# A decoder step on one core: input stage rebuilt, norm factor applied at the copy out, sample rows of v in column groups

## The chip, the cores and the metric

The kernel runs on one core of a Trainium2 chip. The time is that of the device, in microseconds (us), from one execution of the whole program. Engines are TensorE (PE), VectorE (DVE), ScalarE (ACT), GpSimd (POOL) and SyncE (SP), which here only issues DMAs. Times on the timeline are counted from the profiled execution's first instruction.

## The reference, cut to what matters

One step of two decoder layers in fp32, for a prompt of 512 tokens and 8 samples of one token with 1024 cached positions each. Only the start of layer 0 is touched:

```python
hn = rmsnorm(h, norm_mix[0])            # x * rsqrt(mean(x*x) + eps) * gain, 1024 channels
proj = hn @ w_in_ab                     # 1024 x 2048: q, k, v, u, 512 columns each
past_k = cache_k[:, page_table]         # 8 samples x 8 pages of 128 positions, 8 heads x 64
o_sb = stick_breaking_attention(q, [past_k, k], [past_v, v])
pooled = trailing_means(u, widths 2, 4, 8, 16) - u
```

k, v and the last rows of u are outputs too. Then come the output projection, a mixture of 16 experts, a gated embedding, a layer with a convolution of 31 taps (`w_dw`) and a second mixture.

## The kernel before, in words

**Layout.** Channels lie on the 128 partitions: `hT` holds the residual as 8 blocks (`k`) of 128 channels by 520 tokens (512 of the prompt, 8 of the samples). `xnT` holds the normalised one. Large weights and cache pages pass through six ring buffers ("units") of 2 MB. The first 22 units have fixed places: `w_in_ab` for q, k, u, v in buffers 0 to 3, the first two samples' keys in 4 and 5, the next keys in 0, 4, 5, and so on as uses end.

**PSUM.** Work that passes through PSUM is a list of jobs (`dense_plan`), each with the engine that copies it out. Job n uses slot n mod 4, and TensorE's `fill_wait` waits until job n - 4 is copied out. Every engine runs its program strictly in order; engines meet by semaphores.

**Input (before).** SP issues x_prompt in two halves, x_sample, eight page table transfers (each a strided column of 4 B elements for 16 partitions) and the first weight unit, then waits for all twelve small ACT transfers before it issues units 1 to 3. VectorE computes the row numbers for the cache gathers from the page table (L1252 to L1255) and then copies the transposed x out of PSUM (L1260, L1262). TensorE turns x, then the parameter rows and the 31 tap rows (L1816 to L1825).

**Norm (before).** ScalarE squares `hT` block by block into two buffers (L899), VectorE adds (L1236), TensorE sums over partitions (L1782), ScalarE takes the root (L907), VectorE the reciprocal (L1244) and then forms `xnT` = `hT` x gain x factor (L1247). Only then can the products start.

**Projections.** Each of q, k and u is four channel blocks of 8 x 2 products 128x128x260 (L1804), copied out by ScalarE (L890). v is computed with tokens on the output rows (L1872): 16 products of 512 columns for each of two jobs and 8 for the samples' rows. The q rows of the samples are turned, written to DRAM (L709) and read back broadcast over the partitions (L705). For each sample VectorE multiplies the gathered keys with that (L1283) and reduces them (L1286), in the order keys 0 to 4, pooling history and pooling (L1294 to L1301), keys 5 to 7. GpSimd issues the gathers (L683) and the q broadcasts in one program order; each gather waits until the buffer's last user is done.

**Attention.** For each head ScalarE scales the scores, VectorE starts the chain at L1354, GpSimd masks, and TensorE sums the sticks (L1905). `keep_busy` (L1768) are products whose result nobody reads, ahead of some waits.

## Time and profile before

| | us |
|---|---|
| median of 3 runs | 1443.25 (1442.7 to 1445.9) |
| the profiled execution: its time | 1447.69 |
| the profiled execution: its span, first to last instruction | 1445.9 |
| busy: PE, DVE, ACT, POOL | 1338.9, 1015.4, 709.1, 255.2 |
| mean granted TensorE clock | 0.965 |

A busy TensorE is not one at its peak: matmul ends are modelled and overlap. The granted clock is a share of the full 2.4 GHz, so 0.50 is 1.2 GHz. An idle engine costs something only where the chain passes through it.

### The profile page before, as it was taken

Reading aid. Unit: us, or ns where it says so; the run is one execution under the profiler, and the core shown is the slowest. Engines: PE = TensorE matmul, PEld = TensorE weight load, DVE = VectorE, ACT = ScalarE, POOL = GpSimd, SP = SyncE. Lnnn points to the kernel's source line nnn. Section 1 sums busy time; section 2 is a strip of 40 time slices with the busy share of each in tenths; the row PEclk is TensorE's granted clock in tenths of the full one; section 3 lists DMA queues with packets and bytes.
Section 4 is the critical chain, followed back from the end, with each engine's and each line's share of the span. In section 5 each row is a group of like instructions: output and inputs, shape, how many; then the busy total and the mean of one; then the engine's idle time right before and its main releaser. Section 6 shows DMA issues by size and latency. Waiting matters only on the chain.

```text
span 1445.9 us, 16284 instructions
## 1 busy us (share of the span) xinstructions
PE 1338.9 (93%) x6237; PEld 1046.7 (72%) x6238; DVE 1015.4 (70%) x1038; ACT 709.1 (49%) x702; POOL 255.2 (18%) x251
## 2 busy tenths in 40 slices
PE   2899988999799999998999999999789999999897
PEld 2787454687678888887678885478678878887776
DVE  3258955314798888895855999932788888988573
ACT  2010144113577777774542007242467777877364
POOL 2034235300112332221000000100202233221000
PEclk7899999998999999999999999999899999999898
DMA  7539436306589999996542303002479999997401
GB/s 263 197 143 369 183 122 236 116 1 243 189 312 377 308 381 377 375 380 238 189 155 101 117 0 121 3 1 79 140 249 372 388 309 388 385 376 271 173 1 60
DMA packets 122726, 314.07 MB, mean 217 GB/s; under 512 B 10044, under 2 KB 10704, under 8 KB 120592
## 3 DMA queue, kind: packets, MB, share of 16 engines
q1 hardware_dynamic: 106942, 251.95, 48.0%
q0 software_dynamic: 13648, 56.56, 10.9%
q10 hardware_dynamic: 2074, 4.71, 1.0%
q8 instruction: 43, 0.70, 0.2%
q14 instruction: 19, 0.16, 0.0%
HBM read 304.17 MB, written 26.70 MB: 229 GB/s over the span
## 4 chain that ended last, share of the span: by engine, by line
PE 39%; DVE 9%; DMA 2%; issue 1%; ACT 1%; SPq 0%; ACTq 0%; POOLq 0%; DVEq 0%; PEldq 0%
PE ps L1804 12%; PE ps L2038 6%; PE ps L2039 5%; PE ps L2040 5%; DVE arena L1696 4%; PE ps L2192 2%; PE ps L2194 2%; PE ps L2193 2%; PE ps L1760 2%; DMA ring<-in_w_gate_e 2%; DVE ring_parts L1519 1%; DVE hT L1632 1%; PE ps L2309 1%; PE ps L2204 1%; DVE ring L1600 1%
## 5 line engine op out<-in xcount | busy, mean ns | idle before, releaser
L1804 PE MATMUL ps<-xnT,ring 128*128 128x260 f32 x1408 | 313.0, 385 | 7.3 <-DVE xnT L1247 5.1
L1804 PEld LDWEIGHTS ps<-xnT,ring 128*128 128x128 f32 x1408 | 268.5, 191 | 50.5 <-issue 5.8
L2039 PE MATMUL ps<-ring_parts,arena_parts 128*128 128x512 f32 x768 | 304.3, 396 | 0.0
L1519 DVE TENSOR_TENSOR ring_parts<-ring,xnT_parts 128x2048 fp32r<-128x2048 f32 x96 | 218.7, 2290 | 42.9 <-ACT xnT_parts L1012 41.7
L1519 DVE TENSOR_TENSOR ring_parts<-ring,arena_parts 128x2048 fp32r<-128x2048 f32 x96 | 218.9, 2289 | 32.8 <-ACT arena_parts L1012 32.1
L1012 ACT ACTIVATE xnT_parts<-ring 128x2048 fp32r<-128x2048 f32 x96 | 182.6, 1916 | 80.0 <-PE ps L2040 60.2
L1012 ACT ACTIVATE arena_parts<-ring 128x2048 fp32r<-128x2048 f32 x96 | 182.4, 1916 | 62.2 <-PE ps L2040 43.0
L2039 PEld LDWEIGHTS ps<-ring_parts,arena_parts 128*128 128x128 f32 x768 | 146.0, 190 | 30.6
L2038 PE MATMUL ps<-xnT_parts,arena_parts 128*128 128x512 f32 x384 | 155.5, 405 | 7.4 <-DVE arena_parts L1523 7.3
L2038 PE MATMUL ps<-arena_parts 128*128 128x512 f32 x384 | 155.0, 404 | 7.1 <-DVE arena_parts L1545 3.8
L2040 PE MATMUL ps<-xnT_parts,arena_parts 128*128 128x512 f32 x384 | 152.7, 398 | 0.0
L2040 PE MATMUL ps<-arena_parts 128*128 128x512 f32 x384 | 150.9, 393 | 0.0
L788 POOL DMA_INDIRECT y_rows<-arena,tab_i x32 | 65.3, 2039 | 455.2 <-ACT arena L1024 455.2
L1696 DVE SCALAR_TENSOR_TENSOR arena<-arena,wdw 128x512 f32<-128x512 f32 x150 | 112.8, 752 | 6.0 <-DVE arena L1722 0.2
L1760 PE MATMUL ps<-ident,arena 128*128 128x128 f32 (+5 forms) x617 | 84.9, 283 | 28.9 <-DVE hT L1260 10.9
L783 POOL DMA_INDIRECT arena<-x_rows,tab_i x32 | 81.1, 2536 | 167.2 <-DMA x_rows<-arena 82.1
L1760 PEld LDWEIGHTS ps<-ident,arena 128*128 128x128 f32 (+5 forms) x617 | 74.7, 145 | 42.5 <-DVE hT L1260 12.8
L899 ACT ACTIVATE sq<-hT 128x520 f32<-128x520 f32 x56 | 35.1, 633 | 121.8 <-DVE hT L1405 90.2
L2038 PEld LDWEIGHTS ps<-xnT_parts,arena_parts 128*128 128x128 f32 x384 | 72.7, 189 | 25.9 <-DVE arena_parts L1523 9.0
L2038 PEld LDWEIGHTS ps<-arena_parts 128*128 128x128 f32 x384 | 72.8, 190 | 23.8 <-DVE arena_parts L1545 4.3
L2040 PEld LDWEIGHTS ps<-xnT_parts,arena_parts 128*128 128x128 f32 x384 | 72.7, 189 | 17.7
L2040 PEld LDWEIGHTS ps<-arena_parts 128*128 128x128 f32 x384 | 72.7, 189 | 17.2
(309 smaller groups left out, 1709.6 us busy)
## 6 DMA issues: line engine op xcount, KB each, us to landing
ring<-in_w_gate_e SPq DMA_DIRECT2D x32, 2048.0 KB, 18.3
ring<-in_w_up_e SPq DMA_DIRECT2D x32, 2048.0 KB, 17.6
ring<-in_w_down_e SPq DMA_DIRECT2D x32, 2048.0 KB, 18.9
ring<-in_w_in_ab SPq DMA_DIRECT2D x4, 2048.0 KB, 26.3
ring<-in_w_ple_gate SPq DMA_DIRECT2D x4, 2048.0 KB, 8.0
ring<-y_rows SPq DMA_DIRECT2D x16, 512.0 KB, 6.8
ring<-in_w_in_c SPq DMA_DIRECT2D x4, 2048.0 KB, 8.8
x_rows<-arena ACTq DMA_DIRECT2D x10, 416.0 KB
```

The lines of the kernel that those rows point to most:

```text
L783: pool.indirect_dma_start(xg[:, e % GATHERS, :], None, x_rows[layer], bass.IndirectOffsetOnAxis(ap=tab_i[:, 0, e * BLK:e * BLK + 1], axis= ...
L788: pool.indirect_dma_start(y_rows[layer], bass.IndirectOffsetOnAxis(ap=tab_i[:, 1, e * BLK:e * BLK + 1], axis=0), yo[:, e % 2, :], None, bo ...
L899: nc.scalar.activation(sq[:, k % 2, 0:T], src[:, k, :], ACT.Square).then_inc(s_sq, 1)
L1012: nc.scalar.activation(high[hu0 % 4], unit(n)[:, at:at + HU], ACT.Copy).then_inc(s_hi, 1)
L1519: v.tensor_tensor(w_lo, w, high[hu0 % 4].bitcast(F32), ALU.subtract).then_inc(s_lo, 1)
L1696: link(v.scalar_tensor_tensor(y, x, tap, y, ALU.mult, ALU.add))
L1760: return nc.tensor.transpose(dst, src, ident[0:n, 0:n])
L1804: ins = mm(s[:, half, 0:HALF], w[:, k, :], src[:, k, half * HALF:(half + 1) * HALF], start=(k == 0), stop=(k == n - 1))
L2038: mm(ps[:, bank, :], x, w, start=start, stop=False)
L2039: mm(ps[:, bank, :], x, w_lo, start=False, stop=False)
L2040: return mm(ps[:, bank, :], x_lo, w, start=False, stop=stop)
L2192: mm(s[:, 0, :], hi[:, k, cols], gx_hi[:, k, :], start=(k == 0), stop=False)
```

## The change

- The page table comes in one transfer of 256 B, broadcast to all 128 partitions, tenth on the ACT queue. Each partition picks its own page's column with a mask (`own_page`) and a sum, in fp32. This work now stands behind the copies of x on VectorE.
- x_sample goes first on SP's queue and its transposes come first. SP no longer waits before units 1 to 3. The constants that TensorE's transposes need come first on GpSimd.
- ScalarE squares each block as soon as its part of x is copied, into eight buffers (`sq8`); VectorE adds them in three operations. ScalarE also forms `xnT` = `hT` x gain, without the norm factor.
- TensorE starts the first q block on that, and takes the sums of the norm behind it, as columns for all tokens and as a value for each token row (`rtok`). VectorE applies the factor as it copies q, k and u out (`scaled`); ScalarE applies it for v.
- The taps are turned late, ahead of v. VectorE's key steps are split in two and interleaved with the copies. The first u block comes ahead of the k rows.
- The samples' rows of v are computed between the two other v jobs, as 8 products in four groups of 32 output rows, copied and folded by one more product.

```diff
-    order = [("x", i, "dve") for i in range(5)] + [("params", 0, "dve")]
+    order = [("x", i, "dve") for i in (4, 0, 1, 2, 3)] + [("params", 0, "dve")]
...
+    order.append(("q", 0, "dve"))
     norm(0)
-    order += [("q", m, "act") for m in range(4)] + [("qrow", 0, "act")]
-    order += [("k", m, "act") for m in range(4)] + [("krow", i, "act") for i in range(3)]
-    order += [("u", m, "act") for m in range(4)] + [("srow", 0, "act"), ("urow", 0, "dve")]
+    order += [("q", m, "dve") for m in range(1, 4)] + [("qrow", 0, "act")]
+    order += [("k", m, "dve") for m in range(4)] + [("u", 0, "dve")] + [("krow", i, "act") for i in range(3)]
+    order += [("u", m, "dve") for m in range(1, 4)] + [("srow", 0, "act"), ("urow", 0, "dve"), ("taps", 0, "dve")]
...
-        page_of = sb("page_of", [P, TS], I32)
+        page_all = sb("page_all", [P, TS * PAGES], I32)
+        page_f = sb("page_f", [P, TS * PAGES])
...
+        ar = Arena(8400)
+        sq8 = ar(KT, T)
...
+        vxs = shaped(arena[:, 15520:15776], (KT, 32))
+        vpart = arena[:, 12960:13472]
...
-                eng.wait_ge(s_drained["dve"], JOBS[("x", 4)][2])
+                eng.wait_ge(s_drained["dve"], JOBS[("x", k // 2)][2])
...
+            sp.dma_start(x_smp, a["x_sample"][:, 0, :]).then_inc(s_in, 16)
             sp.dma_start(x_tok[:, :, 0:D // 2], x_src[:, :, 0:D // 2]).then_inc(s_in, 16)
             sp.dma_start(x_tok[:, :, D // 2:D], x_src[:, :, D // 2:D]).then_inc(s_rest, 16)
-            sp.dma_start(x_smp, a["x_sample"][:, 0, :]).then_inc(s_rest, 16)
-
-            for g in range(PAGES):
-                sp.dma_start(page_of[SUB * g:SUB * g + SUB, :], a["page_table"][:, g].partition_broadcast(SUB),
-                             allow_slow_non_contiguous=True).then_inc(s_pt, 16)
             load(0)
-            sp.wait_ge(s_in2, 16 * 12)
             for n in range(1, 4):
                 load(n)
...
-            pool.iota(part_of[:], [[0, 1]], base=0, channel_multiplier=1).then_inc(s_part, 1)
             link(pool.memset(ones[:], 1.0))
             link(pool.memset(ident[:], 0.0))
             link(pool.affine_select(out=ident[:], in_=ident[:], compare_op=ALU.not_equal, fill=1.0, base=0,
                                     pattern=[[-1, P]], channel_multiplier=1))
+            link(pool.memset(eps[:], EPS))
+            pool.memset(idx[:], 0).then_inc(s_const, 1)
+            pool.iota(part_of[:], [[0, 1]], base=0, channel_multiplier=1)
...
+                               pattern=[[SUB, PAGES]], channel_multiplier=-1).then_inc(s_part, 1)
...
+            pool.iota(cfix[:], [[0, 4], [1, 16]], base=1, channel_multiplier=0,
+                      allow_small_or_imprecise_dtypes=True).then_inc(s_const, 1)
...
+            pool.memset(vxs, 0.0).then_inc(s_upz, 1)
             pool.dma_start(hist_rows, a["state_pool"][0].rearrange("b r c -> (b r) c")).then_inc(s_hist, 16)
...
-            act.dma_start(dw_rows, a["w_dw"][0]).then_inc(s_in2, 16)
-            act.dma_start(sbb[:], a["sb_bias"][0].partition_broadcast(P)).then_inc(s_in2, 16)
-            act.dma_start(wpool[:], a["w_pool"][0].rearrange("g c d -> c g d")).then_inc(s_in2, 16)
+            act.dma_start(page_all[:], a["page_table"].rearrange("b g -> (b g)").partition_broadcast(P)).then_inc(s_pt, 16)
+            act.dma_start(sbb[:], a["sb_bias"][0].partition_broadcast(P)).then_inc(s_in3, 16)
+            act.dma_start(wpool[:], a["w_pool"][0].rearrange("g c d -> c g d")).then_inc(s_in3, 16)
+            act.dma_start(dw_rows, a["w_dw"][0]).then_inc(s_in3, 16)
...
+            for k in range(KT):
+                h_wait(act, "x", k)
+                nc.scalar.activation(sq8[:, k, :], hT[:, k, :], ACT.Square).then_inc(s_sq, 1)
+            act.wait_ge(s_drained["dve"], JOBS[("params", 0)][2])
+            for k in range(KT):
+                nc.scalar.activation(xnT[:, k, :], hT[:, k, :], ACT.Copy, scale=prm[:, G_MIX + k:G_MIX + k + 1]
+                                     ).then_inc(s_xn, 1)
             act.wait_ge(s_const, 1)
-            norm(0, "x")
-            two = lambda t: t.rearrange("p (a b) -> p a b", a=2)
-            for m in range(4):
-                copy_out("q", m, two(qT[:, m, :]), halves)
+            s = drain_wait(act, "norm", 0)
+            nc.scalar.activation(two(rms[:]), halves(s), ACT.Sqrt, bias=eps[:], scale=MULT)
+            nc.scalar.activation(rtok[:, 0, 0:4], s[:, 0, HALF:HALF + 4], ACT.Sqrt, bias=eps[:], scale=MULT)
+            nc.scalar.activation(rtok[0:TS, 0, 4:5], s[0:TS, 0, HALF + 4:HALF + 5], ACT.Sqrt, bias=eps[0:TS, :], scale=MULT
+                                 ).then_inc(s_drained["act"], 1)
...
-            for m in range(4):
-                copy_out("k", m, two(kT[:, m, :]), halves)
...
-            for m in range(4):
-                copy_out("u", m, two(up[:, m, PAD:PAD + T]), halves)
...
+            act.wait_ge(s_vtok, 1)
             for i in range(2):
-                copy_out("v", i, v_tok[:, 2 * i:2 * i + 2, :], lambda s: s)
-            copy_out("v", 2, v_tok[0:TS, 4, :], lambda s: s[0:TS, 0, :])
+                s = drain_wait(act, "v", i)
+                nc.scalar.activation(v_tok[:, 2 * i, :], s[:, 0, :], ACT.Copy, scale=rtok[:, 1, 2 * i:2 * i + 1])
+                nc.scalar.activation(v_tok[:, 2 * i + 1, :], s[:, 1, :], ACT.Copy, scale=rtok[:, 1, 2 * i + 1:2 * i + 2]
+                                     ).then_inc(s_drained["act"], 1)
+                if i:
+                    break
+                act.wait_ge(s_vgf, 1)
+                s = slot(JOBS[("v", 2)][0])
+                nc.scalar.activation(vpart, s[:, 1, :], ACT.Copy).then_inc(s_vpart, 1)
+            s = drain_wait(act, "v", 2)
+            nc.scalar.activation(v_tok[0:TS, 4, :], s[0:TS, 0, :], ACT.Copy, scale=rtok[0:TS, 1, 4:5]
+                                 ).then_inc(s_drained["act"], 1)
...
+            act.wait_ge(s_const, 2)
+            act.wait_ge(s_in3, 48)
...
-            def norm(i, upd, gain, added=0):
...
-                dve.wait_ge(s_drained["act"], JOBS[("norm", i)][2])
-                link(v.reciprocal(rstd[:], rms[:]))
-                for k in range(KT):
-                    h_wait(dve, upd, k)
-                    v.scalar_tensor_tensor(xnT[:, k, :], hT[:, k, :], prm[:, gain + k:gain + k + 1], rstd[:],
-                                           ALU.mult, ALU.mult).then_inc(s_xn, 1)
...
-            dve.wait_ge(s_part, 1)
-            link(v.tensor_scalar(part_of[:], part_of[:], SUB - 1, None, ALU.bitwise_and))
-            dve.wait_ge(s_pt, 16 * PAGES)
-            link(v.tensor_scalar(cache_row[:], page_of[:], SUB.bit_length() - 1, None, ALU.logical_shift_left))
-            v.tensor_tensor(cache_row[:], cache_row[:], part_of[:].broadcast_to([P, TS]), ALU.add).then_inc(s_rows, 1)
-
-
+            s = drain_wait(dve, "x", 4)
+            v.tensor_copy(hT[:, :, TP:T], s[:, 0, 0:KT * TS].rearrange("p (k c) -> p k c", k=KT)
+                          ).then_inc(s_drained["dve"], 1)
...
-            s = drain_wait(dve, "x", 4)
-            v.tensor_copy(hT[:, :, TP:T], s[:, 0, 0:KT * TS].rearrange("p (k c) -> p k c", k=KT)
-                          ).then_inc(s_drained["dve"], 1)
             s = drain_wait(dve, "params", 0)
-            v.tensor_copy(prm[:], s[:, 1, 0:N_PRM])
-            v.tensor_copy(wdw[:].rearrange("p k c -> p (k c)"), s[:, 1, 128:128 + KT * CW]
-                          ).then_inc(s_drained["dve"], 1)
-            dve.wait_ge(s_const, 1)
+            v.tensor_copy(prm[:], s[:, 1, 0:N_PRM]).then_inc(s_drained["dve"], 1)
...
+            dve.wait_ge(s_part, 1)
+            link(v.tensor_scalar(part_of[:], part_of[:], SUB - 1, None, ALU.bitwise_and))
+            link(v.tensor_copy(part_f[:], part_of[:]))
+            dve.wait_ge(s_pt, 16)
+            link(v.tensor_copy(page_f[:], page_all[:]))
+            by_page = page_f[:].rearrange("p (b g) -> p b g", b=TS)
+            link(v.tensor_tensor(by_page, by_page, own_page[:].unsqueeze(1).broadcast_to([P, TS, PAGES]), ALU.mult))
+            link(v.tensor_reduce(page_of[:], by_page, AX, ALU.add))
+            link(v.scalar_tensor_tensor(page_of[:], page_of[:], float(SUB), part_f[:].broadcast_to([P, TS]),
+                                        ALU.mult, ALU.add))
+            v.tensor_copy(cache_row[:], page_of[:]).then_inc(s_rows, 1)
+
+            dve.wait_ge(s_sq, KT)
+            link(v.tensor_tensor(sq8[:, 0:4, :], sq8[:, 0:4, :], sq8[:, 4:KT, :], ALU.add))
+            link(v.tensor_tensor(sq8[:, 0:2, :], sq8[:, 0:2, :], sq8[:, 2:4, :], ALU.add))
+            v.tensor_tensor(rstd[:], sq8[:, 0, :], sq8[:, 1, :], ALU.add).then_inc(s_sqadd, KT)
+            dve.wait_ge(s_const, 2)
...
-            norm(0, "x", G_MIX)
-
-            def sum_keys(b):
+            dve.wait_ge(s_drained["act"], JOBS[("norm", 0)][2])
+            link(v.reciprocal(rstd[:], rms[:]))
+            v.reciprocal(rtok[:, 1, 0:4], rtok[:, 0, 0:4])
+            v.reciprocal(rtok[0:TS, 1, 4:5], rtok[0:TS, 0, 4:5]).then_inc(s_vtok, 1)
+
+            def scaled(name, m, dst):
+
+                s = drain_wait(dve, name, m)
+                v.tensor_tensor(two(dst), halves(s), two(rstd[:]), ALU.mult).then_inc(s_drained["dve"], 1)
+
+            def weigh_keys(b):
...
-            for b in range(5):
-                sum_keys(b)
+            for m in range(4):
+                scaled("q", m, qT[:, m, :])
+            scaled("k", 0, kT[:, 0, :])
+            weigh_keys(0)
+            scaled("k", 1, kT[:, 1, :])
+            sum_keys(0)
+            scaled("k", 2, kT[:, 2, :])
+            weigh_keys(1)
+            sum_keys(1)
+            scaled("k", 3, kT[:, 3, :])
+            weigh_keys(2)
+            scaled("u", 0, up[:, 0, PAD:PAD + T])
+            sum_keys(2)
+            weigh_keys(3)
+            sum_keys(3)
+            scaled("u", 1, up[:, 1, PAD:PAD + T])
+            weigh_keys(4)
+            scaled("u", 2, up[:, 2, PAD:PAD + T])
+            sum_keys(4)
+            scaled("u", 3, up[:, 3, PAD:PAD + T])
             s = drain_wait(dve, "urow", 0)
-            dve.wait_ge(s_upz, 1)
+            dve.wait_ge(s_upz, 2)
+            v.tensor_copy(vxs[:, :, 0:TS], xnT[:, :, TP:T]).then_inc(s_vxs, 1)
             v.tensor_copy(u_row, s[0:HIST, 0, :])
             v.tensor_copy(hist[:, :, :, 0:HIST], s[:, 1, 0:480].rearrange("p (g b r) -> p g b r", g=4, b=TS)
                           ).then_inc(s_drained["dve"], 1)
+            s = drain_wait(dve, "taps", 0)
+            v.tensor_copy(wdw[:].rearrange("p k c -> p (k c)"), s[:, 1, 128:128 + KT * CW]
+                          ).then_inc(s_drained["dve"], 1)
...
-            dve.wait_ge(s_drained["act"], JOBS[("u", 3)][2])
...
-            sum_keys(5)
-            sum_keys(6)
-            sum_keys(SBH - 1)
+            for b in range(5, TS):
+                weigh_keys(b)
+                sum_keys(b)
...
+                dve.wait_ge(s_in3, 48)
...
             pe.wait_ge(s_const, 1)
+            s = fill_wait(pe, "x", 4)
+            pe.wait_ge(s_in, 32)
+            for k in range(KT):
+                ins = tr(s[:, 0, k * TS:(k + 1) * TS], x_smp[:, k * P:(k + 1) * P], TS)
+            filled(ins)
             for i in range(4):
-                pe.wait_ge(*((s_in, 16) if i < 2 else (s_rest, 32)))
+                if i == 2:
+                    pe.wait_ge(s_rest, 16)
...
-            s = fill_wait(pe, "x", 4)
-            for k in range(KT):
-                ins = tr(s[:, 0, k * TS:(k + 1) * TS], x_smp[:, k * P:(k + 1) * P], TS)
-            filled(ins)
             s = fill_wait(pe, "params", 0)
-            pe.wait_ge(s_in2, 16 * 12)
-            tr(s[:, 1, 0:N_PRM], prm_rows, N_PRM)
-            for k in range(KT):
-                ins = tr(s[:, 1, 128 + k * CW:128 + (k + 1) * CW], dw_rows[:, k * P:(k + 1) * P], CW)
-            filled(ins)
-
-            square_sums("norm", 0)
-
-            def project(name, c, wait=None):
+            pe.wait_ge(s_in2, 16 * 9)
+            filled(tr(s[:, 1, 0:N_PRM], prm_rows, N_PRM))
...
-            project("q", 0, wait=xn_wait)
+            project("q", 0, 0, 1, wait=xn_wait)
+            s = fill_wait(pe, "norm", 0)
+            pe.wait_ge(s_sqadd, 8)
+            for half in range(2):
+                mm(s[:, half, 0:HALF], ones[:], rstd[:, half * HALF:(half + 1) * HALF], start=True, stop=True)
+            for n in range(5):
+                last = min(T, (n + 1) * P)
+                ins = mm(s[0:last - n * P, 0, HALF + n:HALF + n + 1], rstd[:, n * P:last], ones[:, 0:1], start=True, stop=True)
+            filled(ins)
+            sq_seen[0] += 1
+            project("q", 0, 1, 4)
             s = fill_wait(pe, "qrow", 0)
-            pe.wait_ge(s_drained["act"], JOBS[("q", 3)][2])
+            pe.wait_ge(s_drained["dve"], JOBS[("q", 3)][2])
...
-            project("k", 1)
+            project("k", 1, 0, 4)
+            project("u", 3, 0, 1)
             for i in range(3):
...
-            project("u", 3)
+            project("u", 3, 1, 4)
...
+            s = fill_wait(pe, "taps", 0)
+            pe.wait_ge(s_in3, 48)
+            for k in range(KT):
+                ins = tr(s[:, 1, 128 + k * CW:128 + (k + 1) * CW], dw_rows[:, k * P:(k + 1) * P], CW)
+            filled(ins)
...
-            for i in range(3):
+            for i in range(2):
                 s = fill_wait(pe, "v", i)
-                for b in range(2 if i < 2 else 1):
+                for b in range(2):
                     t = 2 * i + b
-                    rows = P if t < 4 else TS
                     for k in range(KT):
-                        ins = mm(s[0:rows, b, :], xnT[:, k, t * P:t * P + rows], w_view(n)[:, k, :],
+                        ins = mm(s[:, b, :], xnT[:, k, t * P:t * P + P], w_view(n)[:, k, :],
                                  start=(k == 0), stop=(k == KT - 1))
                 filled(ins)
+                if i:
+                    break
+                s = fill_wait(pe, "v", 2)
+                pe.wait_ge(s_vxs, 1)
+                for k in range(KT):
+                    g = 32 * (k % 4)
+                    ins = mm(s[g:g + 32, 1, :], vxs[:, k, :], w_view(n)[:, k, :], start=(k < 4), stop=(k >= 4))
+                ins.then_inc(s_vgf, 1)
+            s = slot(JOBS[("v", 2)][0])
+            pe.wait_ge(s_vpart, 1)
+            filled(mm(s[0:TS, 0, :], fold[:, 0:TS], vpart, start=True, stop=True))
...
+            pe.wait_ge(s_const, 2)
...
+            pe.wait_ge(s_in3, 48)
```

## Rows read from the trace of the kernel before

**Rows 1.** The page's chain that ended last, by engine.
```profile
PE 39%; DVE 9%; DMA 2%; issue 1%; ACT 1%; SPq 0%; ACTq 0%; POOLq 0%; DVEq 0%; PEldq 0%
```

**Rows 2.** Windows: each engine's busy us, granted clock, DMA share, GB/s.
```profile
8.50:18.00 9.50, 3.21 (x22) 2.87 (x20) 0.00 (x0) 0.00 (x0) 0.00 (x0) 0.94 0.10 17
18.00:43.00 25.00, 4.48 (x21) 3.23 (x22) 16.79 (x29) 8.13 (x11) 4.10 (x6) 0.50 1.00 395
43.00:60.00 17.00, 16.99 (x67) 14.41 (x68) 4.56 (x7) 1.01 (x2) 0.00 (x0) 0.86 0.72 259
```

**Rows 3.** Timeline, 0 to 75 us: start, length, instruction, count, idle time before it.
```profile
6.06 5.64 PE L1760 MATMUL ps<-ident,arena 128*128 128x128 f32 x32 [6.06 <-DMA arena<-in_x_prompt]
...
21.05 0.17 DVE L1254 TENSOR_SCALAR cache_row<-page_of 128x8 int32<-128x8 int32 x1 [19.60 <-DMA page_of<-in_page_table]
...
21.34 4.61 DVE L1260 COPY hT<-ps 128x1024 f32<-128x1024 f32 x4
...
25.87 0.21 DVE L1262 COPY hT<-ps 128x64 f32<-128x64 f32 x1
...
27.46 1.16 ACT L899 ACTIVATE sq<-hT 128x520 f32<-128x520 f32 x2
...
35.83 2.07 PE L1782 MATMUL ps<-rstd,ones 128*128 128x260 f32 x4 [9.26 <-DVE rstd L1236]
37.94 0.69 ACT L907 ACTIVATE rms<-ps,eps 128x520 f32<-128x520 f32 x1 [1.83 <-PE ps L1782]
38.66 3.40 DVE L1244 RECIPROCAL rstd<-rms 128x520 f32<-128x520 f32 x1 [2.98 <-ACT rms L907]
...
43.01 30.58 PE L1804 MATMUL ps<-xnT,ring 128*128 128x260 f32 x128 [5.11 <-DVE xnT L1247]
52.58 0.60 ACT L890 ACTIVATE arena<-ps 128x520 f32<-128x520 f32 x1 [13.95 <-PE ps L1804]
...
73.62 0.60 ACT L890 ACTIVATE arena<-ps 128x520 f32<-128x520 f32 x1 [6.41 <-PE ps L1804]
```

**Rows 4.** Timelines of VectorE and TensorE, 75 to 340 us.
```profile
87.41 4.43 DVE L1283 TENSOR_TENSOR ring<-ring,arena 128x4096 f32<-128x4096 f32 x1 [39.85 <-DMA arena<-q_rows]
...
136.52 0.68 DVE L1308 COPY arena<-ps 15x512 f32<-15x512 f32 x1 [5.09 <-PE ps L1760]
...
151.75 4.43 DVE L1283 TENSOR_TENSOR ring<-ring,arena 128x4096 f32<-128x4096 f32 x1 [0.22 <-DVE arena L1301]
...
164.75 6.17 PE L1872 MATMUL ps<-ring,xnT 128*8 128x512 f32 x14
...
175.52 2.87 PE L1887 MATMUL ps<-arena 64*128 64x512 f32 x8 [1.50 <-ACT arena L944]
...
178.11 1.48 DVE L1354 SCALAR_TENSOR_TENSOR arena<-arena 128x1280 f32<-128x1280 f32 x1
...
187.18 1.71 PE L1905 MATMUL ps<-arena,tri 128*128 128x512 f32 x2 [2.23 <-POOL xnT L745]
...
192.70 2.42 PE L1887 MATMUL ps<-arena 64*128 64x512 f32 x8
...
339.33 1.05 PE L1792 MATMUL ps<-ones,rstd 128*104 128x1 f32 x10 [0.40 <-DVE rstd L1236]
```

**Rows 5.** DMA queues up to 8.5 us: the ACT queue's packets, MB, share.
```profile
q10 hardware_dynamic: 200, 0.05, 2.7%
```

**Rows 6.** Windows around two idle spells of TensorE.
```profile
13.00:17.00 4.00, 0.00 (x0) 0.00 (x0) 0.00 (x0) 0.00 (x0) 0.00 (x0) 0.99 0.11 21
17.00:18.00 1.00, 0.00 (x0) 0.00 (x0) 0.00 (x0) 0.00 (x0) 0.00 (x0) 0.50 0.20 52
...
187.00:191.00 4.00, 3.82 (x6) 1.98 (x7) 2.39 (x3) 1.37 (x2) 1.16 (x2) 0.57 0.45 123
```

**Rows 7.** Groups by line and form on VectorE: busy us, mean ns.
```profile
L1519 DVE TENSOR_TENSOR ring_parts<-ring,arena_parts 128x2048 fp32r<-128x2048 f32 x96 | 218.9, 2289 | 32.8 <-ACT arena_parts L1012 32.1
...
L1710 DVE TENSOR_TENSOR arena<-ps,rstd 128x520 f32<-128x520 f32 x8 | 5.6, 699 | 5.1 <-PE ps L1804 4.8
```

34 lines of the change are left out of this document (19 added, 15 removed).

## The prediction

> **What bounds the kernel now.** I read four views, in this order. First the chain that ended last [rows 1]: TensorE holds 39% of it, VectorE 9%, DMA 2%. Whatever the change saves can count only where TensorE, or what TensorE waits for, is late. All edits lie ahead of the attention, so I looked at that stretch alone. Cut into stretches [rows 2], it shows something odd near the start: between 8.5 and 18 us the DMA engines move 17 GB/s, then 395 GB/s from 18 to 43 us with TensorE at a mean clock of 0.50. Nothing runs while little is moved.
>
> The timeline tells why [rows 3]. The first 32 transposes of x run from 6.06 us, but VectorE, which must copy them out of PSUM, has its page table work ahead in its queue and sits idle for 19.60 us until the last of eight page table transfers lands (21.05). Only then does it copy; hT is complete at 26.1 (25.87 + 0.21). ScalarE begins its squares after that, the ring of two buffers makes it and VectorE take turns, and a norm in strict order follows: TensorE sums at 35.83, ScalarE's root at 37.94, a reciprocal of 3.40 at 38.66, the products with gain and factor, and the first q product at 43.01. The first channel block is full at 52.58, the fourth at 73.62.
>
> From there a second chain runs to the attention [rows 4]. q goes out as a row to DRAM, comes back broadcast, and VectorE starts on the cached keys at 87.41. It works through five (5 x 8.79 = 43.9, by three taking 178.11 - 151.75 = 26.36), waits 5.09, turns and pools to 151.75, does the other three, and starts the attention at 178.11. TensorE was there earlier: the scaling of its first scores is over and the second ones run at 175.52. So two things matter before the attention: when the fourth q block is full, and what VectorE does afterwards. TensorE's v products have 178.1 - 175.5 = 2.6 us to spare today.
>
> **The change, part by part**, with times of the profiled execution.
>
> *Input.* VectorE no longer stands behind the page table. x_sample goes ahead of x_prompt (32 KB, one issue, some 0.4 us late), and its 8 transposes (1.0) come first. TensorE then has 32 transposes at 5.64/32 = 0.176, four groups of 1.41. With a start at 6.5, the groups fill at about 8.9, 10.3, 11.7 and 13.1; VectorE follows with 1.2 each [rows 3] and hT is complete at 14.35 instead of 26.1: **-11.7**. The nine parameter transfers are no obstacle: the ACT queue had moved 200 packets and 0.05 MB by 8.5 us [rows 5], which are the 100 rows of 512 B with their completions.
>
> *Norm.* Squares go to eight buffers, so ScalarE paces itself: 1.16 for two [rows 3], behind each copy; with a table load of 1.28 that could wait for the first copy it ends at 16.1. The eight gained copies of h follow at 0.58 each, and the first is there at 16.7: that is when q starts, as the factor is now applied at the copy out. From complete hT to q it takes 2.4 instead of 16.9: **-14.5**. VectorE's page arithmetic (7 small operations of 0.2) and its three additions (2.3 for 128x2080 by the 2.29 of 128x2048 [rows 7], then 1.2 and 0.7, with gaps 4.4) lie beside the first q block. They give the sum at about 20.9; TensorE wants it at 23.7 or later, so they cost nothing while the page table lands by 17.5. The cfix work (some 2) lies in the same shade. The root's table load is hidden by TensorE's first block.
>
> *First q block and the sums in it.* 7.0 at full clock (three blocks take 73.62 - 52.58 = 21.0), 9.57 today since the clock was at 0.50 when it began. The clock is my first choice. TensorE is idle from 13.3 to 16.7. Today it went idle at 11.7 and still had 0.99 from 13 to 17, 0.50 from 17 to 18 [rows 6], so by that row 3.4 us idle leave the clock up and the block costs 7.0. Later, however, a stretch with gaps of 2 to 3 us is followed by a mean of 0.57 from 187 to 191. Bounds 0 and 2.4 lost; I take 1.7, nearer the second row, as its gap is the shorter one. Block: 8.7, **-0.9**. TensorE: Matmul & The Clock Gate of the Trainium skill (Part 1) says that the throttled state is the default and that an idle spell brings it back, which speaks against a wait of this length; by it the 2.4 would be lost, by the first row nothing. Behind the block stand the norm sums, 0.9 for the wide ones (half of 2.07, which ran at half clock [rows 3]) and 1.05 for the token sums [rows 4]: **+2.0**.
>
> Root (0.7), two small roots (0.5) and reciprocal (3.4) then end before the second q block does (7.0): the second and third have PSUM slots that wait for nothing of VectorE. Nothing on the path. q is full at 16.7 + 8.7 + 2.0 + 21.0 = 48.4 against 73.6: **-25.1** in all.
>
> *Copies out on VectorE instead of ScalarE.* 0.70 by a product of PSUM with a factor in SBUF [rows 7], against 0.60: +0.1 before the q row. The 13.8 from full q to the first key (73.62 to 87.41 [rows 3, 4]) hold otherwise: the third gather is again issued right before the row. Keys start at 62.4.
>
> *VectorE from there.* Seven copies (k1 to u3) stand between the key steps, 0.65 each with overlap: +4.5. Five keys 43.9, so u3 is out at 110.8; TensorE, with k0 from 49.7, eight blocks of 7.0 and the k rows (2.2), has it full at 108 and idles. srow and urow transposes 1.3; VectorE waits 1.4 where it waited 5.1. Then vxs 0.2, the rows 1.3, the taps 0.4 (the 248 columns moved here), pooling 13.95, three keys 26.4. Sum 92.0 against 178.11 - 87.41 = 90.7: **+1.3**. Attention starts at 154.4, **-23.7**.
>
> *v in column groups.* The samples' rows took 8 products of 128x512, 6.17 for the recorded ones [rows 4], 6.9 in all. Grouped they cost between nothing and that, plus one fold. TensorE is through with v at about 144 and VectorE comes at 154.4, so it is priced at nothing either way; without that cover (10 us) the saving would be some 4.
>
> *Attention.* Everything behind is released by its start and moves along with it; its v gathers and expert loads wait for uses in it. One thing is new: TensorE finishes its fill products and is idle some 6 us before the first stick products (187.18 today, behind 2.2 us idle [rows 4]), and starts them at half clock. Today they take 5.5, to 192.70, with 0.57 for 3.8 of it [rows 6]: some 3.9 at full clock and 7.8 at half, so up to 2.3 more. They lie beside work of ScalarE and VectorE, so I add 0.6 (bounds 0 and 2.3), and 0.3 for the idle at srow (0 to 1.3).
>
> Sum: -25.1 + 0.1 + 1.3 + 0.9 = -22.8. The profiled execution took 1447.69 and would take 1424.9; the median of the three is 1443.25, so **1420.5**.
>
> **DMA under it.** By rows 2 the weights ran at 395 GB/s once the page table was out of the way. Now x (2 MB) is followed at once by w_in_ab, whose first 2 MB are in at some 13 to 15 us, ahead of 16.7. The gathers start near 16.5 and share with units 1 to 3. x, 8 MB of weights, 4 MB of keys and 1.4 MB of states need 39 us at 395, so all are in by 45 (today by 60); unit 1 is wanted at 49.7, unit 3 at 112. A key reaches its slot in time as today.
>
> **The rivals.**
> *Small transfers stay slow (0.13).* If page_all, tenth on the ACT queue and now beside the weight loads, lands at 21 as the page table did, VectorE is held: sum at 27.2 instead of 23.7, 3.6 lost. If the parameters come as late too, ScalarE has no gains before 21 and q starts 5 later. If, further, w_in_ab lands 5 later behind them, nothing adds, it is the same wait. Gain 14 to 19, time 1424 to 1429. For it: the 17 GB/s from 8.5 to 18 [rows 2] hold the ACT queue's last transfers too, so that the page table's shape need not be the only cause. Against: the 200 of rows 5 came through at full load. DMA: Bandwidth & Descriptors of the Trainium skill (Queues, rings and completion order) has each engine alternate between queues by whole packets of several descriptors, so a small transfer beside big ones waits for big packets; by it the page table would come some us late, inside this rival.
> *The gains meet another wait (0.08).* The q row's trip stands behind the third gather; if units 2 and 3 and the states are still moving, keys start up to 6 later, or copies out stand behind late keys in VectorE's order, and TensorE idles for want of slots. Gain 8 to 14, time 1429 to 1435.
> *No change (0.02).* If VectorE's stretch before attention were set by the arrival of keys and not its own work, an earlier start would buy nothing: 1443. Against: its key steps stand back to back.
> *Slower (0.03).* VectorE alone carries keys and copies; if a key arrives late, u copies, urow, pooling and later keys all queue behind it. Each microsecond costs one. It decides from 22.8 us of such delay on; at 26, 1446.5. A gather takes 9 to 13 us and is issued a whole key ahead, so this needs two more gathers' time in a row.
>
> **How the numbers follow.** Forecast 0.74, with its own range 1416 to 1425.5: the three clock terms at nothing (1.7 + 0.6 + 0.3) and 1.5 for what runs of one kernel differ give the lower end, the same terms at their upper bounds (0.7 + 1.7 + 1.0 more) and 1.5 the upper. The range 1415 to 1428 takes in most of the first rival. Faster by over 0.2% (2.9 us, what a measurement here can tell): 0.95; within: 0.02; slower: 0.03.
>
> **What would show it.** VectorE's first copy of x near 7.5 to 9, not 21; squares near 10; first q product at 16.7; second q block at about 27; first key at 62; TensorE idle ahead of srow; attention's first VectorE step at 154; w_in_ab loads at about 400 GB/s from 8.5 us with no trough. Wrong would make it: the page table later than 17.5, q at half clock for more than its first block, gaps between key steps, or a later stage that gets longer.

## The result and the profile after

The changed kernel is faster. The forecast gain was 22.8 us; by the medians it is 14.7 us in the first set of runs, 22.7 in the second and 19.4 in the third.

| set (one chip each) | before, median us (runs) | changed, median us (runs) | ratio, 95% interval |
|---|---|---|---|
| 1, the result | 1444.58 (4) | 1429.84 (1423.68 to 1434.60, 4) | 0.9886 [0.9846, 0.9927] |
| 2 | 1449.21 (1442.32 to 1454.00, 17) | 1426.48 (1424.65 to 1430.99, 6) | 0.9852 [0.9824, 0.9880] |
| 3 | 1448.17 (1442.29 to 1461.57, 17) | 1428.82 (1427.46 to 1437.89, 5) | 0.9848 [0.9808, 0.9888] |

A fourth set, for the kernels warmq, late, pageonly and wrow below, has the kernel before at 1446.83 us (1441.69 to 1454.95, 19) and no run of the changed one.

The forecast was 1420.5 us, a ratio of 1420.5/1443.25 = 0.9842; the result lies 9.3 us above it and 1.8 us above the range's end. The profiled execution has a span of 1432.9 us (time 1434.60; forecast for it 1424.9).

The chain that ended last, of the changed kernel's page, is as [rows 1] but for TensorE's share (39 before) and that of DMA (2 before):
```profile
PE 41%; DVE 9%; ACT 1%; issue 1%; DMA 1%; SPq 0%; ACTq 0%; POOLq 0%; DVEq 0%; PEldq 0%
```
The first stretches, in windows of the changed kernel (columns as in [rows 2]):
```profile
8.50:18.00 9.50, 4.21 (x31) 3.99 (x29) 8.12 (x13) 7.21 (x14) 1.76 (x1) 0.96 0.90 312
18.00:43.00 25.00, 25.00 (x106) 21.34 (x106) 9.60 (x18) 4.80 (x9) 4.36 (x7) 0.88 0.95 367
43.00:60.00 17.00, 16.12 (x76) 13.70 (x75) 1.59 (x3) 0.59 (x1) 1.60 (x2) 1.00 0.70 262
```
Where 17 GB/s moved between 8.5 and 18 us, 312 do now, and TensorE is busy for all of 18 to 43 us. Its timeline, with those of ScalarE and VectorE, beside [rows 3]:
```profile
6.59 6.11 PE L1820 MATMUL ps<-ident,arena 8*128 8x8 f32 x41 [6.59 <-DMA arena<-in_x_prompt]
...
9.51 1.23 DVE L1273 COPY hT<-ps 128x1024 f32<-128x1024 f32 x1 [1.67 <-PE ps L1820]
...
10.77 1.17 ACT L924 ACTIVATE arena<-hT 128x520 f32<-128x520 f32 x2 [2.07 <-DVE hT L1273]
...
17.99 10.26 PE L1864 MATMUL ps<-xnT,ring 128*128 128x260 f32 x32 [5.29 <-DMA ring<-in_w_in_ab]
28.08 1.04 PE L1896 MATMUL ps<-rstd,ones 128*128 128x260 f32 x4
...
51.31 0.70 DVE L1309 TENSOR_TENSOR arena<-ps,rstd 128x520 f32<-128x520 f32 x1 [6.31 <-PE ps L1864]
...
64.67 4.43 DVE L1317 TENSOR_TENSOR ring<-ring,arena 128x4096 f32<-128x4096 f32 x1 [4.17 <-DMA arena<-q_rows]
```
The fourth q block leaves at 51.31 where it was full at 73.62: -22.3. But the first product waited 5.29 us for its weights. Further on, beside [rows 4]:
```profile
112.71 2.07 PE L1820 MATMUL ps<-ident,arena 128*8 128x128 f32 x20 [1.66 <-DVE arena L1309]
...
144.43 1.02 PE L1957 MATMUL ps<-arena,fold 128*8 128x512 f32 x2
...
156.11 1.48 DVE L1414 SCALAR_TENSOR_TENSOR arena<-arena 128x1280 f32<-128x1280 f32 x1
...
165.18 2.08 PE L1988 MATMUL ps<-arena,tri 128*128 128x512 f32 x2 [3.73 <-POOL xnT L755]
...
231.21 3.55 PE L2002 MATMUL ps<-arena 128*64 128x512 f32 x16 [2.19 <-POOL arena L739]
...
260.25 6.78 PE L1864 MATMUL ps<-arena,wpool 128*128 128x260 f32 x16 [1.80 <-DVE xnT L1456]
```
The attention starts at 156.11 us against 178.11, 22.0 us earlier. The same two places, the third group of value products and the pooling projection's first products, in TensorE's timeline of the kernel before:
```profile
253.25 2.37 PE L1919 MATMUL ps<-arena 128*64 128x512 f32 x16 [2.21 <-POOL arena L729]
277.18 3.74 PE L1804 MATMUL ps<-arena,wpool 128*128 128x260 f32 x16 [1.70 <-DVE xnT L1396]
```
and the windows behind them in the changed kernel, at a clock near one half:
```profile
231.00:242.50 11.50, 11.29 (x34) 6.71 (x35) 2.98 (x2) 2.82 (x3) 2.85 (x9) 0.55 0.45 171
260.00:267.00 7.00, 6.75 (x17) 5.41 (x18) 2.28 (x3) 0.00 (x0) 4.24 (x10) 0.54 0.18 13
```
The pooling projection starts only 16.9 us earlier, and its 16 products take 6.78 us where 3.74 stood. So 5.1 us went inside the attention and 3.0 right behind it. The rest of the program adds some 0.9 more, net.

Cut at the attention's first VectorE step and the pooling projection's first product, the four profiles of each kernel that I had in the end read (us; the rest is the span less the two):

| profile | start of attention | start to pooling projection | rest |
|---|---|---|---|
| before, first | 178.1 | 99.1 | 1168.7 |
| before, b1, b2, b3 | 179.4, 177.8, 178.8 | 100.7, 99.1, 99.2 | 1166.5, 1167.3, 1167.3 |
| changed, first | 156.1 | 104.1 | 1172.7 |
| changed, same, same2, same3 | 156.3, 155.6, 155.9 | 104.1, 107.4, 99.2 | 1168.9, 1173.2, 1164.0 |

The start is steady within 1.7 us in either kernel. What comes after it varies by 17 us in the changed kernel and by 1.5 in these four of the kernel before. In the first profile 8.1 of the 9.8 us by which the span misses the forecast lie there. Over four profiles against four the start is 22.5 us earlier, and 4.2 us of that go again before the pooling projection and 2.3 behind it.

### The profile page after: what moved, and what is told of

The parts are those of the page before. It is cut to its first block, busy times and chain, and to the rows that moved or that the text cites. A ratio compares the mean times of both kernels' runs of the same rounds, so it can differ in the third digit from the quotient of the medians.

```text
span 1432.9 us, 16303 instructions
## 1 busy us (share of the span) xinstructions
PE 1341.3 (94%) x6249; PEld 1049.6 (73%) x6250; DVE 1018.2 (71%) x1045; ACT 707.6 (49%) x703; POOL 241.2 (17%) x254
## 4 chain that ended last, share of the span: by engine, by line
PE 41%; DVE 9%; ACT 1%; issue 1%; DMA 1%; SPq 0%; ACTq 0%; POOLq 0%; DVEq 0%; PEldq 0%
PE ps L1864 12%; PE ps L2123 6%; PE ps L2124 6%; PE ps L2125 6%; DVE arena L1756 4%; PE ps L2277 2%; PE ps L2279 2%; PE ps L2278 2%; PE ps L1820 2%; DVE ring_parts L1579 1%; DVE hT L1692 1%; PE ps L2394 1%; PE ps L2289 1%; DVE ring L1660 1%; DMA ring<-y_rows 0%
## 5 line engine op out<-in xcount | busy, mean ns | idle before, releaser
L2123 PE MATMUL ps<-xnT_parts,arena_parts 128*128 128x512 f32 x384 | 155.9, 406 | 8.4 <-DVE arena_parts L1583 8.0
L1820 PE MATMUL ps<-ident,arena 128*128 128x128 f32 (+6 forms) x617 | 83.7, 281 | 17.1 <-DMA arena<-in_x_prompt 6.6
L1820 PEld LDWEIGHTS ps<-ident,arena 128*128 128x128 f32 (+6 forms) x617 | 74.1, 144 | 30.1 <-POOL cfix L682 6.2
L910 ACT ACTIVATE sq<-hT 128x520 f32<-128x520 f32 x48 | 30.2, 633 | 122.5 <-DVE hT L1465 93.3
```

The source lines that it names most:

```text
L910: nc.scalar.activation(sq[:, k % 2, 0:T], src[:, k, :], ACT.Square).then_inc(s_sq, 1)
L1820: return nc.tensor.transpose(dst, src, ident[0:n, 0:n])
L2123: mm(ps[:, bank, :], x, w, start=start, stop=False)
```

## The experiments

### TensorE's clock in the attention: same, busy, bbusy, plainv (set 2)

Theory 1 in the expectations below is that the loss is TensorE's clock, theory 2 that it is a fixed wait. **same** is the changed kernel again.

> The changed kernel as it stands, timed again. Theory 1 (the loss behind the start of the attention is TensorE's clock, which falls in the idle spell ahead of the values or of the pooling projection in some executions and not in others): the executions fall into two groups some 8 to 10 us apart (1423.7 and 1425.8 against 1433.9 and 1434.6 so far), the slower group at a lower mean granted clock (0.966 against 0.974). In a trace of the faster group the stretch that lay at 232 to 243 us runs at full clock. Theory 2 (the loss is a wait that is always there, in the attention, the copies out or the transfers): one group, and the shift against the kernel before falls from -22 us to -14 us in every trace, whatever the clock.

1426.48 us, the six between 1424.65 and 1430.99: no two groups, so that picture of the first four runs was wrong. The mean clock of a run (0.971 to 0.973) did not order the six either. Its trace has the loss all the same, 104.1 us for the stretch.

**busy**, in three places:
```diff
-                    keep_busy(ps_flat[:, c0:c0 + 256], 12)
+                    keep_busy(ps_flat[:, c0:c0 + 256], 20)
...
-                pe.wait_ge(s_wm, 2 * p + 2)
                 if p:
                     pe.wait_ge(s_ot, p)
+                if p < 3:
+                    keep_busy(ps[:, 6, 0:256], 5)
+                pe.wait_ge(s_wm, 2 * p + 2)
...
             pe.wait_ge(s_ot, 4)
+            keep_busy(ps[:, 6, 0:256], 4)
```

> The changed kernel with products of the ones matrix that nothing reads in the idle spells of TensorE in the attention: 20 in place of 12 ahead of the first cumulative sums (the engine idled 3.73 us there), 5 ahead of each of the first three value products (2.19 us of idle time ahead of the third) and 4 ahead of the pooling projection (1.80 us). Theory 1: the clock no longer falls at 232 and 260 us, the start of the pooling projection stays at some -21 us against the kernel before, the executions lie near 1421 to 1426 us, and the mean granted clock is 0.974 or more. Theory 2: no more than 1 us from the changed kernel, in either group. If the added products themselves lie in the way, slower by up to 3 us.

1430.04 us (1428.58 to 1431.87, 6), ratio 0.9879 [0.9852, 0.9907]: no faster, where 1421 to 1426 was expected. But the traces decide between the theories. The last part of the stretch (from 48 us behind the attention's start to the pooling projection, the same work everywhere) in windows, first the changed kernel:
```profile
204.11:260.25 56.14, 49.42 (x276) 27.29 (x275) 24.52 (x29) 17.89 (x14) 18.10 (x53) 0.90 0.58 217
```
the first profile of before:
```profile
226.11:277.18 51.07, 46.12 (x280) 25.42 (x280) 24.60 (x29) 17.90 (x14) 18.18 (x53) 1.00 0.64 239
```
and busy:
```profile
204.80:256.39 51.59, 51.20 (x305) 30.03 (x305) 24.86 (x29) 17.96 (x15) 18.12 (x53) 1.00 0.65 239
```
VectorE, ScalarE and GpSimd have the same busy time in all three. At a mean clock of 1.00 the work takes 51.1, at 0.90 56.1 us; with the added products it stays at 1.00 and takes 51.6. One profile at 1.00 could be luck, since five of the fifteen profiles without added products have it too; but all three with them do (busy, bbusy, best). What the profiles at 1.00 have in common follows with b1 to b3. The whole stretch is 4.5 us shorter in busy. Part of that it gave back: at 497.70 us ScalarE waited 5.96 us for an expert's gate weights, against 3.40 in the changed kernel (the part on the experts' weights). Everything behind the pooling projection's start took 1170.5 us, within the changed kernel's 1164.0 to 1173.2, so the trace does not say why the median is no lower.

**bbusy**: the same edits in the kernel before, without the 20.

> The kernel before with the 5 and 4 added products ahead of the values and ahead of the pooling projection (the 12 ahead of the first cumulative sums unchanged). Its profiled execution kept full clock from 226 to 341 us with the same idle spells (2.21 and 1.70 us). Theory 1: the added products find nothing to save there, 1442 to 1446 us, within 1 us of the kernel before. Theory 2, the same. If the kernel before also loses the clock there in some executions, some 3 to 5 us faster in the median.

1450.23 us (12), ratio 1.0014 [0.9995, 1.0034]. The stretch took 101.6 us: the added products take 2.4 us ahead of each value group, and ahead of the first two TensorE had only 1.61 and 1.05 us of idle time in the first profile of before. GpSimd's steps behind each come some 1.2 us later. Nothing was gained, as both theories had it.

**plainv**: the sample rows of v as 8 products of xnT in one group.
```diff
-                    ins = mm(s[g:g + 32, 1, :], vxs[:, k, :], w_view(n)[:, k, :], start=(k < 4), stop=(k >= 4))
-                ins.then_inc(s_vgf, 1)
...
-            filled(mm(s[0:TS, 0, :], fold[:, 0:TS], vpart, start=True, stop=True))
+                ins = mm(s[0:TS, 0, :], xnT[:, k, TP:T], w_view(n)[:, k, :], start=(k == 0), stop=(k == KT - 1))
+            filled(ins)
```

> The changed kernel with the values of the sample tokens made as in the kernel before: 8 products of 16 rows of xnT in one group, in place of two rounds in four column groups and the fold that waits for ScalarE. The prediction's step: TensorE is done with v about 10 us before VectorE is ready for the attention, so the start of the attention stays at 156.1 us and the time within 1 us of the changed kernel. Rival: the column groups save about 1 us of TensorE's work and the attention starts that much later. By theory 1, moving TensorE's work by a microsecond may also move it from one group of times to the other, in either direction.

The trace: v is done at 148.9 us in place of 145.5 (7.03 us of products for 1.92 and 1.02), and the attention starts at 155.57. The groups save TensorE 3.4 us that nobody waits for, as forecast. The median is 1429.93 (1425.07 to 1434.55, 6), ratio 0.9885 [0.9855, 0.9915], which overlaps same's interval.

### The early terms: warmq, late, pageonly, order, waitnorm

**warmq**, products that nothing reads ahead of the first q block:
```diff
+                    s = fill_wait(pe, "q", 0)
+                    for _ in range(9):
+                        mm(s[:, 0, 0:256], ones[:], x_tok[:, 0, 0:256], start=True, stop=True)
                 unit_wait(pe, n)
```

> The changed kernel with 9 products of the ones matrix on x_tok, which nothing reads, ahead of the first q block, in the 5.3 us in which TensorE waited for the weights of w_in_ab with its clock falling. Theory (the block took 10.3 us in place of the 8.7 of the sum because 17.2 to 24.0 us ran at half clock): the block takes some 7.0 us, the first key and the attention's first VectorE step come 3 us earlier than in the changed kernel (153 in place of 156 us). Rival (the block is set by the copies of xnT that come by ScalarE, eight of 5.05 us in all from 15.5 us, or by the VectorE steps behind it): no more than 1 us at the attention's start. The time itself moves by the same 3 us or less, and the spread of executions (1424.7 to 1434.6 us so far) may hide it.

TensorE's timeline of warmq:
```profile
13.61 4.07 PE L1891 MATMUL ps<-arena,ones 128*128 128x256 f32 x18
18.27 7.28 PE L1864 MATMUL ps<-xnT,ring 128*128 128x260 f32 x32 [0.59 <-DMA ring<-in_w_in_ab]
```
The block takes 7.28 in place of 10.26; it begins 0.3 later and the attention starts at 154.87, 1.2 earlier than in the changed kernel. The block's price was the clock's; less than half reaches the attention, where 3 us was expected, and I have not traced where the rest goes. Median 1427.38 (4), ratio 0.9855 [0.9819, 0.9891], no different from the changed kernel.

**late**, these three moved from the start to behind ScalarE's copies to xnT:
```diff
+            act.dma_start(sbb[:], a["sb_bias"][0].partition_broadcast(P)).then_inc(s_in3, 16)
+            act.dma_start(wpool[:], a["w_pool"][0].rearrange("g c d -> c g d")).then_inc(s_in3, 16)
+            act.dma_start(dw_rows, a["w_dw"][0]).then_inc(s_in3, 16)
```

> The changed kernel with three of its small input transfers (the sb_bias broadcast, w_pool, w_dw) issued by ScalarE behind its copies of xnT, in place of ahead of them. Theory (these small packets beside the bulk load take the transfer rate from some 400 to 80 to 230 GB/s between 9.7 and 13 us, and so w_in_ab's first unit lands at 17.9 us in place of 13 to 15): the rate holds near 400 GB/s, the first q product starts at 15.5 to 16.5 us (then with the first xnT tile at 16), and the attention starts 1 to 2 us earlier. Rival (the page table with its 128 short rows and the params rows cause the trough, or the rate is that of the bulk load alone): first q product within 0.5 us of 17.99.

The rate of all transfers from 8.5 to 18 us in 40 slices, of the changed kernel:
```profile
GB/s 358 420 393 334 318 224 193 209 181 167 174 96 79 96 228 210 233 262 292 362 351 356 401 412 384 375 420 403 369 395 358 377 384 358 386 371 388 405 388 379
```
the same of late:
```profile
GB/s 373 388 382 359 392 255 167 178 125 213 272 316 332 357 367 397 414 405 414 414 405 414 414 405 414 405 405 380 414 397 379 388 362 405 379 388 397 379 388 405
```
and TensorE's timeline of late:
```profile
17.47 8.94 PE L1864 MATMUL ps<-xnT,ring 128*128 128x260 f32 x32 [3.65 <-ACT xnT L924]
```
The trough is shallower (125 GB/s at its lowest, not 79) and shorter: 4 slices below 250 GB/s where there were 12, of 0.24 us each. The first 2 MB of w_in_ab land 14.6 us after their issue, not 15.6, and are no longer what the product waits for. So these three transfers held the weights back by about 1 us. The product starts at 17.47, though, only 0.5 us earlier, where 15.5 to 16.5 was expected: x was turned 0.9 us later in this execution (from 7.46, not 6.59), and `xnT` is now the last to come. The shorter block (8.94 for 10.26) gives the rest of the 1.5 us by which the attention starts earlier, at 154.63. What is left of the trough belongs to the parameter rows, the page table or something else; I did not part them. Median 1426.90 (4), ratio 0.9846 [0.9807, 0.9886], no different from the changed kernel.

**pageonly**: the kernel before, VectorE's page table steps moved behind its copies of x.
```diff
-            dve.wait_ge(s_pt, 16 * PAGES)
-            link(v.tensor_scalar(cache_row[:], page_of[:], SUB.bit_length() - 1, None, ALU.logical_shift_left))
-            v.tensor_tensor(cache_row[:], cache_row[:], part_of[:].broadcast_to([P, TS]), ALU.add).then_inc(s_rows, 1)
```

> The kernel before with one edit: VectorE's wait for the page table and its two steps on it stand behind the copies of x, in place of ahead of them. Everything else of the change is left out (eight transfers for the table, norm factor ahead of the copies, taps, v). By the prediction's term for the input part, 11.7 us: the copies of x start at 9 us in place of 21.05, the first q product at 31 to 32 in place of 43.01, the attention's first VectorE step at 166 to 167 in place of 178.11, and the time is about half of the whole change's gain, 1433 to 1438 us beside 1443 to 1449. If the clock's phase in the attention takes back 3 to 8 us in this kernel too, 1436 to 1445. Rival (the page table or the weights are late in any case): the first q product no earlier than 38 us.

A miss: first q product at 40.88 us, where 31 to 32 was expected, attention at 176.32, only 1.8 us earlier, 1448.14 us (12), ratio 1.0000 [0.9976, 1.0023]. VectorE's timeline of pageonly says why:
```profile
8.89 1.23 DVE L1257 COPY hT<-ps 128x1024 f32<-128x1024 f32 x1 [7.43 <-PE ps L1760]
...
20.91 0.17 DVE L1262 TENSOR_SCALAR cache_row<-page_of 128x8 int32<-128x8 int32 x1 [6.21 <-DMA page_of<-in_page_table]
...
24.49 0.26 DVE L1265 COPY prm<-ps 128x100 f32<-128x100 f32 x1 [3.21 <-PE ps L1760]
```
The copies moved from 21.34 to 8.89, but the additions of the squares still stood behind two waits, for the table and for the parameters (24.49).

**order**, the additions put ahead of the page table steps (moved as in pageonly) and of the params copy:
```diff
+            for k in range(KT):
+                add_square(0, k)
...
-            norm(0, "x", G_MIX)
+            norm(0, "x", G_MIX, added=KT)
```

> The kernel before with VectorE's order changed alone: the copies of x, then the eight sums of squares, and only then the page table, the params copy and cfix. In the run before this one only the page table was moved, and the sums of squares still stood behind the params copy, for which VectorE waited until 24.5 us. Theory (the prediction's input term of 11.7 us was the page table and the params steps together, ahead of the sums on VectorE): the sums of squares end at 22 to 23 us, TensorE's norm sums start at 24 to 25 in place of 35.83 behind the params product (23.1 us, which waits for w_pool), the first q product at 31.5 to 32.5 in place of 43.01, and the attention's first VectorE step 11 us earlier. Time 1435 to 1441 us beside 1442 to 1454. Rival: the small transfers alone, or another wait on VectorE, hold the first q product at 38 us or later.

TensorE's timeline of order:
```profile
24.19 2.10 PE L1784 MATMUL ps<-rstd,ones 128*128 128x260 f32 x4
31.95 18.41 PE L1806 MATMUL ps<-xnT,ring 128*128 128x260 f32 x71 [5.66 <-DVE xnT L1247]
```
First q product 11.1 us earlier, attention at 167.39, 10.7 earlier; 1437.79 us (12), ratio 0.9937 [0.9909, 0.9965]. VectorE's order alone gives half of the change at the attention's start.

**waitnorm**, the changed kernel with the norm sums first:
```diff
-            project("q", 0, 0, 1, wait=xn_wait)
...
-            project("q", 0, 1, 4)
+            pe.wait_ge(s_vtok, 1)
+            project("q", 0, 0, 4, wait=xn_wait)
```

> The changed kernel with TensorE's norm sums ahead of the first q block and q held back until VectorE's reciprocals are done, as the kernel before had it; the factor is still applied at the copy out. Sums at 21.3 us, root and reciprocals until some 28 us, first q product at 28 in place of 17.99. Theory (TensorE's q, 31 to 33 us of work, runs beside the root and the reciprocal, and that overlap is what the norm's term is): the four q blocks end at 56 to 59 us, the fourth q comes out 5 to 8 us later than 51.31, and so does the attention's start (161 to 164 us in place of 156.1). Rival (VectorE and ScalarE set the time of the first keys anyway): less than 2 us.

TensorE's timeline of waitnorm:
```profile
30.78 19.48 PE L1864 MATMUL ps<-xnT,ring 128*128 128x260 f32 x76 [6.10 <-DVE rtok L1304]
```
Attention at 167.27, 11.2 us later than in the changed kernel; I had expected 5 to 8, having started q at 28 and let its blocks end too early. 1436.92 us (4), ratio 0.9896 [0.9855, 0.9938]. The two halves, 10.7 (order) and 11.2 (waitnorm), make up the 22.0; the other edits move the attention's start by next to nothing.

### The experts' weights, and all of it together: wrow, best, same2

In the first layer of experts ScalarE waits, in the changed kernel's timeline, for an expert's gate weights:
```profile
501.36 3.72 ACT L1041 ACTIVATE arena_parts<-ring 128x2048 fp32r<-128x2048 f32 x2 [3.40 <-DMA ring<-in_w_gate_e]
```
Some 20 us earlier, windows of the changed kernel:
```profile
478.00:482.00 4.00, 4.00 (x19) 3.22 (x18) 3.27 (x2) 3.52 (x3) 3.70 (x4) 1.00 0.94 317
482.00:486.00 4.00, 4.00 (x23) 3.38 (x22) 3.67 (x3) 3.13 (x3) 0.72 (x1) 1.00 1.23 280
486.00:490.00 4.00, 4.00 (x22) 3.25 (x21) 3.85 (x3) 2.40 (x2) 0.00 (x0) 1.00 0.67 98
490.00:494.00 4.00, 4.00 (x19) 3.23 (x18) 3.52 (x3) 3.99 (x4) 1.36 (x1) 1.00 0.73 106
```
The rate drops to 98 GB/s behind two transfers of the routing weights (2 KB each in elements of 4 bytes), and TensorE later stands for 1.70 us, at 508. The first profile of before has no such wait for gate weights, though its rate drops to 100 GB/s at the same place of the program (502 to 506 us). Nor has same3. So the low rate by itself does not bring the wait; in these two the loads had room to spare, I take it, which no run shows.

**wrow**, those two moved from the fifth expert to the first:
```diff
+                    if e == 0:
+                        pool.wait_ge(s_tab, routed + 2)
+                        for k in range(2):
+                            pool.dma_start(w_rows[layer][k].rearrange("(i r) -> r i", r=RT), wts[:, k, :],
```

> The changed kernel with the two transfers of the routing weights to DRAM, 528 packets of 4 bytes in all, issued behind the first expert's scatter in place of behind the fifth's. In the traces so far TensorE loses 2.9 us there (5.4 us in the kernel with added products): the transfer rate is at some 100 GB/s for 8 to 12 us behind these transfers and those of p_prompt, and ScalarE waits 3.4 us (6.0 us) for an expert's gate weights at 501 us. Theory (the small packets cause the trough, and the experts' weights are then late): the trough moves to the first expert, the wait at 501 us is gone, and the step of 2.9 us in the shift at 506 to 512 us with it. It may come back at the first expert, where the ring is as full. Rival (p_prompt, left in place, causes it): the wait at 501 us stays.

Slower: 1437.28 us (8), ratio 0.9923 [0.9894, 0.9952]. The low rate came with the transfers, 98 and 56 GB/s from 416 to 424 us, and from 480 to 500 us it was 376 GB/s. The wait for gate weights came at 427.84 (4.46 us) in place of 501.36, and then ScalarE waited for the up weights at every expert, 5.02 us at 492.05. So these packets do cause a trough, and a ring that is behind early stays behind. The wait at 501 went, but its cost came back at more experts.

**best**: warmq, late and busy's products, those ahead of the values only at p = 2.

> The changed kernel with what the runs so far favoured: the three small transfers behind the xnT copies (it brought the attention 1.5 us forward), 9 unread products ahead of the first q block (1.3 us), and unread products in the idle spells: 20 in place of 12 ahead of the first cumulative sums, 5 ahead of the third value product alone, 4 ahead of the pooling projection. Attention's first VectorE step at 153 to 154.5 us, the shift against the kernel before -23 to -25 us until the pooling projection and -23 at 300 us. Then the experts' weights take back 2 to 6 us at 506 us as in every trace with an early start. Median 1421 to 1426 us. Rival (the time is set by the transfers of the experts' weights, so that any gain ahead of them is given back): 1426 us or more, as the changed kernel.

Its trace does most of what was expected: attention at 154.34, the last part of the stretch at a clock of 1.00, span 1422.0. But that part took 52.8 us, 1.2 more than in busy, and the pooling projection starts 22.0 us ahead of the first profile of before, not 23 to 25. The first value products, which best left without added ones, took 4.01 us behind 3.29 us of idle time, against 2.37 in the changed kernel, and all of GpSimd's steps behind them come 1.6 us later. Timed, 1430.71 us (1423.70 to 1432.40, 5), ratio 0.9858 [0.9821, 0.9895], against 0.9848 [0.9808, 0.9888] for the changed kernel beside it. It is not faster than the changed kernel.

**same2**, the changed kernel beside it.

> The changed kernel once more, beside the other three on one chip. Its executions spread over 1424.7 to 1434.6 us so far in ten. Theory (TensorE's clock takes a different part of the early gain in each execution): again a spread of 6 to 10 us; in its trace the shift against the kernel before is -21.5 to -22.2 us at the attention's start, and whatever is lost until the experts start is lost where the granted clock is at one half. Rival: a loss of over 1 us between 160 and 340 us where the clock is full.

Spread 1427.46 to 1437.89, and the profiled one, 1437.89, shows the loss at its largest; its last part of the stretch:
```profile
203.59:263.00 59.41, 52.69 (x276) 29.00 (x275) 24.47 (x29) 17.89 (x14) 18.10 (x53) 0.86 0.55 205
```

### Does the kernel before lose it too: b1, b2, b3, same3

> The kernel before, unchanged, profiled again. In the traces so far the stretch from the attention's start to the pooling projection (160 to 300 us of the first profile of before) is longer than in that first profile by an amount that goes with the time at half clock in it: 13.7 us at half clock and 0 in that profile; 20.5 us and 1.8; 24 us and 5.0; 31 us and 8.1; 34 us and 10.0. Theory (the loss is a state of TensorE's clock that the kernel before has as well, and the one profile on which the prediction rests happened to have none of it): of three further profiles of before at least one shows 2 us or more of the loss, with over 17 us at half clock, and the mean loss of the three is near that of the changed kernel's three profiles (5 to 10 us). Rival (the change brings the loss, by what it does to the waits ahead of the attention): all three within 1 us of the first profile, with 14 us at half clock.

> The same as the run before this one, a second time: theory, over three such profiles a mean loss of 2 us or more between 160 and 300 us and a spread of several us; rival, none in any of them.

> The same, a third time. If the three and the first profile hold losses like those of the changed kernel, the difference between the two kernels is the shift of the attention's start, some 22 us less what the experts' weights take back (2 to 3 us at 506 us, which the first profile of before does not show either); if they hold none, it is that less the mean loss, 14 us.

> The changed kernel, profiled once more on the same chip. Attention's first VectorE step at 155.5 to 156.5 us, and behind it by theory and rival alike a loss of 0 to 10 us that goes with the time at half clock, as in its three profiles so far (8.1, 5.1 and 10.0 us).

The last part of the stretch in b1, the largest of the three (b2 and b3 have 51.06 and 51.16 us at 1.00):
```profile
227.43:280.11 52.68, 46.06 (x276) 24.99 (x275) 24.51 (x29) 17.90 (x14) 18.14 (x53) 0.97 0.62 232
```
in same3, whose time is 1420.83 us (the kernel before beside it 1449.37):
```profile
203.91:255.05 51.14, 46.10 (x280) 25.40 (x280) 24.58 (x29) 17.89 (x14) 18.12 (x53) 1.00 0.64 238
```
and in pageonly, which is the kernel before in all its attention:
```profile
224.32:283.73 59.41, 52.76 (x277) 29.12 (x275) 24.55 (x29) 17.90 (x14) 18.17 (x53) 0.86 0.55 205
```
The same work takes 51.1 to 51.2 us at 1.00, 52.7 at 0.97, 54.3 at 0.93 (order), 56.1 at 0.90 and 59.4 at 0.86, whichever kernel it is.

Something that goes before tells the profiles apart. The ten microseconds from 40 to 50 us behind the attention's start, in the changed kernel's first profile:
```profile
196.11:206.11 10.00, 8.75 (x50) 5.15 (x46) 5.92 (x6) 5.12 (x4) 6.32 (x16) 1.00 0.36 128
...
209.19 0.64 PE L2002 MATMUL ps<-xnT,arena 128*64 128x512 f32 x1 [2.73 <-POOL arena L739]
```
and in same3:
```profile
195.91:205.91 10.00, 8.75 (x34) 5.69 (x30) 5.92 (x6) 5.12 (x4) 6.32 (x16) 0.83 0.35 125
...
208.99 0.64 PE L2002 MATMUL ps<-xnT,arena 128*64 128x512 f32 x1 [1.06 <-POOL arena L739]
```
In same3 the clock is at one half for a part of this window. That costs nothing, since TensorE only idles less behind it: 1.06 us ahead of the second group of value products in place of 2.73. Of the fifteen profiles without added products in the attention, five have 0.83 here and idle 1.05 or 1.06 us there, and all five keep 1.00 to the pooling projection (before, b2, b3, same3, waitnorm). The other ten have 1.00 here and idle 2.73 to 2.75 us, and all ten fall to half clock later and lose 1.6 us or more. The later idle spells, 2.2 and 1.8 us, are the same in all fifteen. So the loss goes with that longer spell, and busy, which fills it, has none. No kernel changes this spell alone, so the cause is not shown.

My theory's number for b1 to b3, a mean loss of 2 us or more, was not met (1.6, 0.0 and 0.1). The rival, that only the change brings the loss, is not met either: same3 has none of it, and pageonly as much as same2, the most. Another part of the first profile of before did prove unusual: b1, b2 and b3 all have the wait for gate weights, as ScalarE's timeline of b1 shows (3.27 us in b3):
```profile
518.84 3.72 ACT L1012 ACTIVATE arena_parts<-ring 128x2048 fp32r<-128x2048 f32 x2 [3.28 <-DMA ring<-in_w_gate_e]
```

## Why the prediction was right and wrong

The direction and the early mechanism held; the time was outside the range. For the profiled execution the forecast is 9.8 us short in span: 1.7 at the attention's start, 4.2 between it and the pooling projection (5.1 where 0.9 was allowed), 3.9 behind (1172.7 less 1168.7 where nothing was allowed).

**Where it failed: the attention.** "Everything behind is released by its start and moves along with it", with a clock term of 0.6 (bounds 0 and 2.3) at the first stick products. That place was fine: its products took 6.6 us where 5.5 stood, and nothing behind them came later. The clock fell elsewhere, behind idle spells of 2.19 and 1.80 us at 231 and 260 us that the kernel before has as well (2.21 and 1.70) without a fall in its first profile. What differs there is the spell ahead of the second value products, 2.73 us against 1.05. In same2 and pageonly it fell one group of value products earlier as well, in the same pattern. The term measured 5.1 in the result's profile, 0.1 to 8.3 over four, and up to 3.0 more in the pooling projection. I took one execution's clock in the attention as the kernel's, and bounded the term by one place.

**Behind the attention** the sum had nothing. ScalarE waits 2.5 to 6.0 us for an expert's gate weights at some 500 us (520 in b1 to b3) in fourteen of the eighteen profiles. The first of before, order and same3 lack it, and in wrow it moved; here too one execution stood for all. The cause of the larger variation of the rest, 1164.0 to 1173.2 us, stays open. It is not in one place: against same3, the first profile of the changed kernel loses 3.5 us by 322 us, where the clock was at one half in the pooling projection, 1.3 near 500 and 3.4 behind 1280 us.

**Input, -11.7.** Right for the whole of it: hT is complete at 14.4 (14.35); order gives 10.7 at the attention. The page table alone, by which the prediction explained the late copies, is worth 1.8 (pageonly), since the additions of the squares stood behind the parameters too.

**Norm, -14.5.** q started at 17.99, not 16.7: w_in_ab's first unit was put at 13 to 15 us at 400 GB/s, and landed at 17.9 behind the trough. That is the first rival's cause with another victim: the page table landed in time, 5.8 us after its issue, and the weights were late. late shows that three of the small transfers account for about 1 us of this; the other 2 to 4 are not explained. The Trainium skill (DMA: Bandwidth & Descriptors, Queues, rings and completion order) says that each engine alternates between queues by whole packets. The prediction drew from it that the small transfer waits for the big ones; here the big one was the one that came too late.

**First q block, 8.7.** 10.26: full loss of the clock and more, where I took 1.7 of 2.4. The idle spell was 5.3, not 3.4 us, since the weights were late; 17.99 to 24.0 ran at half clock. warmq's 7.28 agrees with the 7.0 at full clock. The rule of the Trainium skill (TensorE: Matmul & The Clock Gate, Part 1) that an idle spell brings the throttled state back would have been the better guide here; in the attention the traces show spells of 2.2 us both with and without a fall behind them.

**Sums, +2.0, copies, +0.1, VectorE's stretch, 92.0.** Sums 1.9. First key to attention 156.11 - 64.67 = 91.4. Right. The root's table load was not hidden by the first block, as the prediction had it: it ran at 30.12, behind the sums, and cost nothing: TensorE's products ran on without a gap from 29.96 to 51.3.

**v in column groups, 0.** Right, and plainv confirms it. But the cover was 5.8 us, not the 10 of the prediction: behind v stand the first scores and ScalarE's scaling of them, which ends at 150.3, and the attention starts at 156.1.

**The range** took 1.5 us for what runs differ. Seventeen to nineteen runs of the kernel before span 12 to 19 us, with medians of 1446.8 to 1449.2, so the three that I had (1442.7 to 1445.9) were at the low end. That part of the absolute miss is luck of the draw. As a ratio the forecast, 0.9842, lies inside the intervals of sets 2 and 3 and just outside that of set 1.

What stays open: whether the longer idle spell ahead of the second value products is what makes the clock fall, what decides about the brief half clock ahead of it in a given execution, and whether the earlier start makes the loss likelier. Four profiles against four (5.1, 5.1, 8.3, 0.1 against 0.0, 1.6, 0.0, 0.1) lean that way. The other kernels whose attention is unedited do not settle it: plainv, warmq, late and wrow, which start it at 155 to 157 us, lost 1.8, 1.8, 1.8 and 3.4; waitnorm, order and pageonly, which start it at 167 to 176, lost 0.1, 3.3 and 8.3. They are too few.

## What to carry to other kernels

One profiled execution is one draw of TensorE's clock: before an "everything else moves along", look for the idle spells of 2 us that the later stages have, and put a term of their own in the range for each, even where the profile at hand shows full clock. Half clock where TensorE has time to spare can cost nothing. Transfers issued together share the engines: moving three small ones behind the bulk load that is needed first brought it in 1 us earlier (late), but moving two others to where the ring had no slack cost some 10 us (wrow). And when a long wait is moved in an engine's order, look what stands behind the next one: pageonly gained 1.8 us and order 10.7.

## What was not expected of the hardware

- The same 51 us of attention took five different lengths (51.1, 52.7, 54.3, 56.1, 59.4 us) that go with the mean granted clock (1.00, 0.97, 0.93, 0.90, 0.86). At 0.86, 2 x 0.14 x 59.4 = 16.6 us ran at half clock and 8.3 were lost: half of it. The first has 1.05 us of idle time ahead of the second value products, all the others 2.7.
- With small transfers of 0.33 MB in all beside a bulk load (340 of 2150 packets under 512 B) the rate fell from some 400 to 79 GB/s at its lowest, and with three of them moved to 125 and for a third of the time; two 2 KB transfers of single elements went with some 100 GB/s for 8 us, wherever they were issued.
- ScalarE's table load ran at 7.42 us, well ahead of the first square at 10.77; the prediction had let it wait for the first copy of x. The next one, for the root, did stand behind its wait (30.12 us).
